# Decoder trunk on one core: the chunked RWKV recurrence with one engine loop for its inverses and a scan over chunk states

## The reference, cut to what matters

```python
def step(s, inp):
    r_t, w_t, k_t, v_t, a_t, b_t = inp
    sa = jnp.einsum('nhvk,nhk->nhv', s, a_t)
    s = s * w_t[:, :, None, :] + sa[..., None] * b_t[:, :, None, :] + v_t[..., None] * k_t[:, :, None, :]
    return s, jnp.einsum('nhvk,nhk->nhv', s, r_t)
...
mu_y = jnp.mean(y, axis=-1, keepdims=True)
var_y = jnp.mean(jnp.square(y - mu_y), axis=-1, keepdims=True)
y = ((y - mu_y) * lax.rsqrt(var_y + RWKV_GN_EPS)).reshape(n, t, RWKV_W)
y = y * lp['rwkv_ln_w'] + lp['rwkv_ln_b']
...
y_rwkv = ((y + bonus.reshape(n, t, RWKV_W)) * g).astype(h.dtype)
```

## Time and profile before

| what | us |
|---|---|
| median of three runs | 2193.56 |
| profiled execution, its own time | 2205.53 |
| its span | 2203.7 |
| PE busy | 2126.8 (97%) |
| first gram, to first product of the output projection | 1192.74 to 1318.54 |

### The profile page before, as it was taken

How to read it: one execution, slowest core, us unless ns; L and a number is a source line. 1 busy time by engine, 2 the same in 40 slices (tenths; PEclk the granted TensorE clock), 3 DMA queues, 4 the chain that set the end, 5 groups by cost and what they waited for, 6 DMA issues and landing times.

```text
span 2203.7 us, 46115 instructions
## 1 busy us (share of the span) xinstructions
PE 2126.8 (97%) x19116; PEld 2095.9 (95%) x19116; DVE 1191.8 (54%) x1232; ACT 857.5 (39%) x954; POOL 194.6 (9%) x158
## 2 busy tenths in 40 slices
PE   6999999999999999999987889999999999999997
PEld 5999999999999999999985779999999999999997
DVE  5555555555455454769766446555555555544442
ACT  4444444444344343443323114444444444433332
POOL 3000000000000010044104720100000000000000
PEclk9999999999999999999997859999999999999998
DMA  5555555555555556587850105655555555555552
GB/s 158 183 180 182 180 181 181 181 180 182 172 182 188 174 186 189 163 224 230 255 160 9 32 24 175 188 180 180 178 185 179 183 179 181 182 165 194 189 170 97
DMA packets 359032, 373.52 MB, mean 169 GB/s; under 512 B 13329, under 2 KB 351797, under 8 KB 358742
## 3 DMA queue, kind: packets, MB, share of 16 engines
q1 hardware_dynamic: 349280, 348.17, 49.7%
q0 software_dynamic: 5920, 17.48, 3.1%
q10 hardware_dynamic: 3742, 6.52, 0.9%
HBM read 366.82 MB, written 5.32 MB: 169 GB/s over the span
## 4 chain that ended last, share of the span: by engine, by line
PE 91%; DVE 5%; DMA 2%; ACT 1%; issue 1%; ACTq 0%; POOL 0%; SPq 0%; POOLq 0%; DVEq 0%
PE ps L305 28%; PE ps L307 28%; PE ps L306 28%; DMA raw<-in_w_in_dram 2%; DVE wL L292 1%; PE ps L1066 1%; PE ps L1394 1%; PE ps L1609 1%; PE ps L1582 1%; PE ps L1678 0%; DVE xL L339 0%; PE ps L1601 0%; ACT wH L286 0%; PE ps L1665 0%; PE ps L1760 0%
## 5 line engine op out<-in xcount | busy, mean ns | idle before, releaser
L292 DVE TENSOR_TENSOR wL<-raw,wH 128x1024 fp32r<-128x1024 f32 (+1 forms) x676 | 828.4, 1231 | 864.1 <-ACT wH L286 863.8
L286 ACT ACTIVATE wH<-raw 128x1024 fp32r<-128x1024 f32 (+1 forms) x676 | 699.9, 1037 | 1013.5 <-PE ps L307 948.2
L305 PE MATMUL ps<-xH,wH 128*128 128x264 f32 x3616 | 1031.8, 285 | 12.6 <-DVE wL L292 12.6
L307 PE MATMUL ps<-xH,wL 128*128 128x264 f32 x3616 | 1029.7, 285 | 0.0
L306 PE MATMUL ps<-xL,wH 128*128 128x264 f32 x3616 | 1029.5, 285 | 0.0
L305 PEld LDWEIGHTS ps<-xH,wH 128*128 128x128 f32 x3616 | 683.9, 189 | 14.6 <-issue 13.9
L307 PEld LDWEIGHTS ps<-xH,wL 128*128 128x128 f32 x3616 | 683.5, 189 | 0.0
L306 PEld LDWEIGHTS ps<-xL,wH 128*128 128x128 f32 x3616 | 683.0, 189 | 0.2
L305 PE MATMUL ps<-hH,wH 128*128 128x264 f32 x1408 | 402.4, 286 | 0.0
L307 PE MATMUL ps<-hH,wL 128*128 128x264 f32 x1408 | 401.4, 285 | 0.0
L306 PE MATMUL ps<-hL,wH 128*128 128x264 f32 x1408 | 401.3, 285 | 0.0
(11 more groups left out here) (331 smaller groups left out, 1219.2 us busy)
## 6 DMA issues: line engine op xcount, KB each, us to landing
raw<-in_ffn_w_gate_dram SPq DMA_DIRECT2D x176, 512.0 KB, 3.4
raw<-in_ffn_w_up_dram SPq DMA_DIRECT2D x176, 512.0 KB, 3.5
raw<-in_ffn_w_down_dram SPq DMA_DIRECT2D x128, 512.0 KB, 3.5
raw<-in_w_in_dram SPq DMA_DIRECT2D x100, 512.0 KB, 4.8
raw<-in_ffn_w_down_dram SPq DMA_DIRECT2D x64, 384.0 KB, 3.1
raw<-in_w_out_dram SPq DMA_DIRECT2D x32, 512.0 KB, 4.6
kb<-in_cache_swa_k_dram POOLq DMA_DIRECT2D x24, 256.0 KB, 6.5
vb<-in_cache_swa_v_dram ACTq DMA_DIRECT2D x24, 256.0 KB, 5.4
```

Of the source, the lines that this page charges most:

```text
L286: nc.scalar.activation(wH[:, k % RING, 0:nk, :], raw[:, k % RING, 0:nk, :], ACT.Copy).then_inc(S("head_made"), 1)
L292: nc.vector.tensor_tensor(wL[:, k % RING, 0:nk, :], raw[:, k % RING, 0:nk, :], wH[:, k % RING, 0:nk, :].bitcast(F32), ALU.subtract).then_i ...
L305: nc.tensor.matmul(out, wH[:, k % RING, q, cols], high, start=a, stop=False)
L307: last = nc.tensor.matmul(out, wL[:, k % RING, q, cols], high, start=False, stop=b)
```

## The change

- `inner` is one tile whose slots replace the separate tiles, since the loop needs fixed places and one product takes two of them side by side as its right operand.
- The levels become `with pe.Fori(0, LEVELS)` on TensorE alone; the other engines' level code stays unrolled. X is no longer kept by a product and a masked copy: every level TensorE transposes Z (6 transposes of 128x128) and VectorE copies the result.
- The chunk walk becomes: multiply the inverse with [own values | a by token] (`pe_solved`), form for chunks 1 to 3 a matrix that takes the incoming state to reads and to the next state (`pe_transition`), and then scan the states (`pe_state`) and write outputs for two chunks at a time (`pe_outputs`).
- Group norm has two parts. The gain is multiplied into the spread matrix `hs` once (GpSimd), the bias is added to the bonus by ScalarE, and both gates are on VectorE, in PSUM.
- GpSimd forms the sample output from the old state (one product by w r, and two dot products that VectorE reduces) before it updates the state. `ycat` and `sample_y` are now GpSimd's.

```diff
+    Zq = Wq = inner_slots(0, 1)
+    Aak = Fq = inner_slots(2, 3)
+    Xq = [m.rearrange("p (i t) c -> p i t c", t=2) for m in inner_slots(4, 7)]
+    FQ_AT, TOKA_AT = (2, 3), (5, 6)
+    toka = inner_slots(*TOKA_AT)
+    Aq = inner_slots(8, 9)
+    Qq = inner_slots(10, 11)
+    UV = inner_slots(12, 13, 14) + [last_uv[:]]
+    KB_AT, AR_AT = (11, 8, 9, 10), (5, 4, 7, 6)
+    KB, AR = inner_slots(*KB_AT), inner_slots(*AR_AT)
+    states = [inner[:, k:k + RT, :] for k in (2 * H, 2 * H + RT, 3 * H)] + [ST[:]]
+    LR = at("LR", [P, 3, RT, 2 * C], F32, PB)
...
+        pool.dma_start(lnwr[:], t["rwkv_ln_w"].broadcast_to([H, RW])).then_inc(S("rwkv_tables_in"), 16)
...
+        g.tensor_tensor(ycat[:], sv[:, 2:4, :], sv[:, 4:5, :].broadcast_to([96, 2, C]), ALU.mult
+                        ).then_inc(S("sample_parts"), 1)
+        step(g.tensor_tensor(sv[:, 0, :], sv[:, 1, :], sv[:, 4, :], ALU.mult))
+        pool.wait_ge(S("sample_sums"), 1)
         step(g.tensor_tensor(S2[:], S1[:], key(0), ALU.mult))
         halve()
         step(g.tensor_tensor(S1[:], S1[:], key(1), ALU.mult))
-        pool.wait_ge(S("sample_sums"), 1)
+        pool.wait_ge(S("sample_sums"), 3)
+        for value, dot in ((smal[:, 0:C], smal[:, C:C + 1]), (sv[:, 5, :], smal[:, C + 1:C + 2])):
+            step(g.tensor_scalar(ycat[:, 0, :], value, dot, None, ALU.mult))
+            step(g.tensor_tensor(smy[:], smy[:], ycat[:, 0, :], ALU.add))
+        for a in range(2):
+            g.tensor_scalar(ycat[:, a, :], smy[:], cgat[:, 48 + a:49 + a], None, ALU.mult).then_inc(S("sample_y"), 1)
...
+    def pe_inverse(pe):
+        pe.wait_ge(S("decayed"), 2)
+        pe.wait_ge(S("tokens_staged"), 5)
+        pe_gram(pe, bT, aT, 0, 0)
+        pe_gram(pe, aT, bT, 0, 4)
+        pe.wait_ge(S("tokens_staged"), 6)
+        pe_gram(pe, bT, aT, 1, 2)
+        pe_gram(pe, aT, bT, 1, 6)
+        pe.wait_ge(S("decayed"), 4)
+        for n in range(2):
+            pe.wait_ge(S("grams_out"), 2 * n + 1)
+            pe_gram(pe, pkr, aT, n, 4 + 2 * n)
+        with pe.Fori(0, LEVELS) as lv:
+            for n in range(2):
+                pe.wait_ge(S("grams_out"), 2 * n + 2)
+                pe.wait_ge(S("z_level"), lv * 2 + (n + 1))
+                for i in range(RT):
+                    pair = Zq[n][:, 2 * i:2 * i + 2, :].rearrange("p b c -> p (b c)")
+                    last = nc.tensor.transpose(wide(slice(0, P), 4 + 2 * n, i), pair, ident)
+                last.then_inc(S("level_x"), 1)
+                for i, b, cp in every():
+                    last = nc.tensor.matmul(place(HALF[b], 2 * n + cp, i), Aq[n][HALF[cp], slot(b, i), :],
+                                            Zq[n][HALF[cp], 2 * i + b, :], start=True, stop=True)
+                last.then_inc(S("level_q"), 1)
+            for n in range(2):
+                pe.wait_ge(S("grams_out"), 4)
+                pe.wait_ge(S("level_q_out"), lv * 2 + (n + 1))
+                pe.wait_ge(S("level_x_out"), lv * 2 + (n + 1))
+                for i, b, cp in every():
+                    last = nc.tensor.matmul(place(HALF[cp], 2 * n + b, i), Xq[n][HALF[b], i, cp, :],
+                                            Qq[n][HALF[b], slot(cp, i), :], start=True, stop=True)
+                last.then_inc(S("level_z"), 1)
...
+    def pe_solved(pe, m, first):
         for i, b, cp in every():
...
+            R = HALF[cp]
+            rhs = side_by_side(R, FQ_AT[m] * H + slot(b, i), TOKA_AT[m] * H + 2 * i + b)
+            last = nc.tensor.matmul(wide(HALF[1 - cp], first, 2 * i + b), Zq[m][R, 2 * i + b, :], rhs,
+                                    start=True, stop=True)
+        last.then_inc(S("solved"), 1)
+    def pe_turn_keys(pe, n, first):
+        c = chunk(n)
+        for i in range(RT):
+            low, high = (bT, pkr) if n % 2 else (pkr, bT)
+            nc.tensor.transpose(wide(HALF[0], first, i), low[:, i, c], ident)
+            last = nc.tensor.matmul(wide(HALF[1], first, i), high[:, i, c], ident, start=True, stop=True)
+        last.then_inc(S("tokens_turned"), 1)
+    def pe_reads(pe, n, first):
+        c = chunk(n)
+        for i in range(RT):
+            for k in range(4):
+                b, own = k % 2, k // 2 ^ k % 2
+                last = nc.tensor.matmul(place(HALF[n % 2 if own else 1 - n % 2], first + b, i),
+                                        (pkr if own else bT)[HALF[b], i, c], pr[HALF[b], i, c], start=True, stop=True)
+        last.then_inc(S("grams_made"), 1)
+    def pe_transition(pe, n, first):
+        m, R = n // 2, HALF[1 - n % 2]
+        for i, b in both():
+            rhs = side_by_side(R, AR_AT[n] * H + slot(b, i), KB_AT[n] * H + 2 * i + b)
+            last = nc.tensor.matmul(wide(HALF[b], first, i), Wq[m][R, 2 * i + b, :], rhs, start=True, stop=True)
+        last.then_inc(S("transitions"), 1)
+    def pe_state(pe, n, bank):
+        for i, b in both():
+            h, out = 2 * i + b, place(HALF[b], bank, i)
+            last = nc.tensor.matmul(out, KB[n][:, h, :], UV[n][:, h, :], start=True, stop=n == 0)
+            if n:
+                last = nc.tensor.matmul(out, LR[HALF[b], n - 1, i, C:2 * C], states[n - 1][HALF[b], i, :],
+                                        start=False, stop=True)
+        last.then_inc(S("states_made"), 1)
+    def pe_outputs(pe, m, first):
+        for n in (2 * m, 2 * m + 1):
+            for i, b in both():
+                h, k = 2 * i + b, i % 3 * P + n % 2 * C
+                out = ps[HALF[b], first + i // 3, k:k + C]
+                last = nc.tensor.matmul(out, UV[n][:, h, :], AR[n][:, slot(b, i), :], start=True, stop=n == 0)
+                if n:
+                    last = nc.tensor.matmul(out, states[n - 1][HALF[b], i, :], LR[HALF[b], n - 1, i, 0:C],
+                                            start=False, stop=True)
+        last.then_inc(S("outputs"), 1)
...
+        pe_own_values(pe, 0, 4)
+        pe_own_values(pe, 1, 6)
+        pe.wait_ge(S("z_level"), 11)
+        pe_reads(pe, 1, 0)
+        pe.wait_ge(S("z_level"), 12)
+        pe_turn_keys(pe, 1, 2)
+        pe.wait_ge(S("tokens_staged"), 8)
+        pe_solved(pe, 0, 4)
+        pe.wait_ge(S("tokens_staged"), 9)
+        pe_turn_keys(pe, 0, 2)
+        pe.wait_ge(S("grams_out"), 5)
+        pe.wait_ge(S("tokens_staged"), 10)
+        pe_solved(pe, 1, 0)
+        pe.wait_ge(S("solved_v"), 3)
+        pe.wait_ge(S("solved_a"), 3)
+        pe_transition(pe, 1, 4)
+        pe_state(pe, 0, 7)
+        pe.wait_ge(S("solved_v"), 6)
+        pe.wait_ge(S("solved_a"), 6)
+        pe_reads(pe, 2, 0)
+        pe_turn_keys(pe, 2, 2)
+        pe.wait_ge(S("transitions_out"), 1)
+        pe.wait_ge(S("states_out"), 1)
+        pe_state(pe, 1, 6)
+        pe_reads(pe, 3, 4)
+        pe.wait_ge(S("tokens_staged"), 11)
+        pe_turn_keys(pe, 3, 2)
+        pe.wait_ge(S("grams_out"), 6)
+        pe_transition(pe, 2, 0)
+        pe.wait_ge(S("tokens_staged"), 12)
+        pe_reads(pe, 0, 2)
+        pe.wait_ge(S("transitions_out"), 2)
+        pe.wait_ge(S("states_out"), 2)
+        pe_state(pe, 2, 7)
+        pe.wait_ge(S("grams_out"), 7)
+        pe_transition(pe, 3, 4)
+        pe.wait_ge(S("grams_out"), 8)
+        pe_outputs(pe, 0, 0)
+        pe.wait_ge(S("transitions_out"), 3)
+        pe.wait_ge(S("states_out"), 3)
+        pe_outputs(pe, 1, 4)
+        pe_group_sums(pe, 0)
+        pe_state(pe, 3, 1)
+        pe.wait_ge(S("sample_y"), 2)
+        nc.tensor.matmul(ps[:, 7, 408:456], ycat[:].rearrange("p a e -> p (a e)"), cgat[:, 0:48],
+                         start=True, stop=True).then_inc(S("sample_turned_y"), 1)
+        pe_group_squares(pe, 0)
...
-        nc.vector.tensor_tensor(tiles(pvr, part), tiles(pvr, part), group_bank(part), ALU.mult
...
+        dve.wait_ge(S("gates_out"), 18 + RT)
+        link(v.tensor_tensor(out, out, tiles(pvr, part), ALU.mult), dve)
+        link(v.tensor_tensor(out, out, tiles(bv, part), ALU.add), dve)
+        v.tensor_tensor(out, out, tiles(gg, part), ALU.mult).then_inc(S("rwkv_made"), 1)
...
+        keys(0)
+        keys(1)
+        solved(0)
+        solved(1)
+        keys(2)
+        keys(3)
...
+        act_group_squares(act, 0)
+        act_group_root(act, 0)
         act_group_squares(act, 1)
         act_group_root(act, 1)
...
+        act_rwkv_head(act, 0)
+        act_rwkv_head(act, 1)
         act.wait_ge(S("sample_state_out"), 16)
```

```diff
         for lv in range(LEVELS):
             for n in range(2):
+                dve.wait_ge(S("level_x"), 2 * lv + n + 1)
+                v.tensor_copy(Xq[n].rearrange("p (g i) t c -> p g (i t c)", g=2), ps[:, 4 + 2 * n:6 + 2 * n, 0:384]
+                              ).then_inc(S("level_x_out"), 1)
+            for n in range(2):
                 dve.wait_ge(S("level_z"), 2 * lv + n + 1)
...
+                dve_level(dve, 2 * (lv + 1) + n)
             if lv == 1:
-                dve_sample_sums(dve, 1)
+                dve.wait_ge(S("sample_parts"), 1)
```

(25 more changed lines are left out.)

483 lines of the change are left out of this document (149 added, 334 removed).

## The result

The changed kernel takes 2229.89 us (median of 4, 2228.79 to 2230.43), the kernel before 2191.62 in the same session (2188.53 to 2202.67). The ratio is 1.0165, with a 95% interval from 1.0128 to 1.0201: it is slower, since the whole interval lies above 1. The forecast was 2169.6, the range 2160 to 2194; both missed. The profiled execution took 2229.53 us, its span is 2227.8. One thing is needed to read the numbers: of 21 executions of the kernel before in the first session of experiments, 17 took 2186.6 to 2196.2 us and 4 took 2205.4 to 2207.1, and the one that was profiled before (2205.53) is like those four.

The account below looks back on a forecast made before the run. TensorE, busy for 97% of the span, was taken as the bound; levels 17 us less, chunks 33 us for 50, and the output projection's shift less 2 us kept back gave 24 us gain: 2169.6 us, range 2160 to 2194.

Parts of the forecast that it names:

- The grams and the levels: Inverse stage: no gain in grams, levels start at 1200, 5.8 to 5.9 us each, end at 1230.5; 17 us less.
- rival 3: Levels' loop: clock falls there too, 9.9 us a level, on top of a slow chunk stage; 2216, slower; chance 0.06.
- Rival 2: Levels' loop: code is fetched again at each back edge, 14 us; gain 10, total 2184; chance 0.06.
- The Trainium skill's rule on taken branches: Levels' loop: a taken branch with its target outside the two pages held stalls for a fetch; rows spoke against it.
- The chunks: Chunk stage: batches priced by rows, sum 32.3 us and 1 of waits, 33 in place of 50; outputs end at 1263.7.
- The keys: Chunk stage, six transposes beside six products: 1.6 us a batch taken, 2.3 if in turn; four batches, 6.4 us.
- The last state: Group norm stage: the last state was priced at 2.6 us, at half clock.
- The clock: Full clock forecast for the chunk stage, since batches alternate halves or use all rows; half clock for the norm.
- rival 1: Chunk stage: clock stays at half, 32.3 us grow by 25, 2193, chance 0.10; in part 2176 to 2190, chance 0.20.
- The norm and GpSimd: After the outputs: norm chain ends at 1293.4, GpSimd's at 1294.1, so together; first output product at 1294.3.
- The base: Whole kernel: gain of 24 us from the profiled 2205.5 us, carried over to the median 12 us below it: 2169.6.
- rival 4: Chunk stage: keys and solved at their lower bounds, GpSimd's and the norm's chains 3 us forward; 2165; chance 0.06.

Follow-up runs that it names:

- a1: Changed kernel with the 64-row product ahead of the 128-row one for every second head in states and outputs; 2188.33 us, ratio 0.9976 to the kernel before.
- a4: a3 with each keys batch issued as six transposes and then six products, instead of in turn; 2179.54 us, ratio 0.9921 to the kernel before.
- b2: Changed kernel without accumulation in states and outputs, same order of products (other numbers computed); 2229.46 us, ratio 1.0162 to the kernel before.
- b5: a4 with VectorE's sum for the sample ahead of its second solved copies, two weight heads and a tail earlier; 2173.52 us, ratio 0.9912.
- d1: b5 with each keys batch made of twelve plain products in turn on the two column halves; 2172.45 us, ratio 0.9906 to the kernel before.
- d3: Changed kernel with products grouped in runs by row size in the states alone, outputs still in turn; 2202.74 us, ratio 1.0032 to the kernel before.
- b4: a4 with the five levels of the inverse unrolled in TensorE's program instead of looped; 2179.21 us, ratio 0.9933 to the kernel before.
- b1: Changed kernel with products on the state before replaced by repeats of the 128-row products in states and outputs (other numbers computed); 2182.83 us, ratio 0.9952.
- a3: Changed kernel with products in runs by row size, four in the states and up to eight in the outputs; 2181.82 us, ratio 0.9945.

## Why the prediction was wrong, point by point

**The grams and the levels: right in their times, not in the reason.** Start 1197.7 (forecast 1200), passes 5.4 to 6.3 us apart (5.8 to 5.9), end 1226.9 (1230.5). The clock stayed at 1.00 with transposes busy for 8.7 of the 29.2 us, so rival 3 did not come. It is no flat rule: in six of the other kernels (a1, a4, b2, b5, d1, d3) the clock was 0.50 for 6.8 us from about 1198, over the start of the levels, and rose with the same transposes under way (a4: 0.50 from 1199.3 to 1206.1, then 1.00). The groups of the changed kernel that answer to the earlier trace rows, from 1195 to 1228:

```profile
L1625 PE MATMUL ps<-inner 64*64 64x64 f32 x480 | 9.3, 222 | 0.0
L1633 PE MATMUL ps<-inner 64*64 64x64 f32 x480 | 9.0, 220 | 2.2 <-issue 1.3 <-ACT inner L1846 0.9
L1622 PE MATMUL ps<-cb,inner 128*128 128x128 f32 x60 | 8.7, 282 | 0.7 <-DVE inner L1892 0.3 <-issue 0.2
```

Rival 2 did not come either: 1.5 us of issue waits in five passes, and 4 instruction packets from 1200 to 1250. The Trainium skill's rule on taken branches (the page and section named in the prediction) gives no visible cost here, and unrolling (b4) is no slower. Of the 18.9 us by which the stage is shorter, 10.5 are TensorE's busy time (36.8 to 26.3) and 8.4 its idle time (11.3 to 2.9). In the busy time, 60 transposes (8.7 us) stand for 192 products (13.1 us), and grams that were busy for some 6 us between the levels have moved to other stages. Why the idle time went is not shown; my reading of it as code that arrives late was not borne out.

**The chunks: the step that failed.** "States 0.8 and twice 1.5, outputs 2.2 and 2.9, from 30 to 34 ns a row as in own values." The states took 0.9, 7.0 and 9.7, the outputs 30.4. Own values is a batch of one size, and the price held wherever the batch had one size (b1: 1.66 and 5.17). It did not hold for products in turn between 128 and 64 rows. Against the forecast of 1263.7 the outputs ended at 1310.2, 46.5 us late: states 13.8 (17.6 for 3.8), outputs 25.3, keys 10.2 (16.6 for 6.4), and all the rest -2.8. The keys failed in the same way; I took the lower of two prices because the two kinds "use different columns", and only plain products do so with gain. The last state, which stands in the norm, failed once more: 9.75 us for the 2.6 forecast.

**The clock: wrong, as a consequence.** "The new chunk stage alternates halves or uses all rows in nearly every batch. So I take the full clock for it." It fell at about 1253, inside state 1, and was 0.50 until about 1328. With runs of two (a1) it did not fall in this stage. The outputs end at 1310.2 there and at 1270.7 in a3, 39.5 us apart. Up to that point a3 has 34 changes fewer in the states and 61 in the outputs; 95 at 0.20 us are 19 us of drains, and the other 20 are the lower clock, on the drains and on all between them. This is rival 1's condition, but it scaled a sum without drains and came to 2193. One reading behind the choice was also off. Of the 14 us at 0.50 that the prediction calls products on 64 or fewer rows, 3.4 were products on all 128 rows (groups of the kernel before, 1160 to 1174):

```profile
L1394 PE MATMUL ps<-pj,lora 128*128 128x264 f32 x7 | 3.4, 670 | 0.0
```

Nor do changes of size explain every fall: the chunk walk of the kernel before was at 0.50 for 38 us with nearly all its products of 64x64. What brings the clock down in general stays open; shown is that in this stage grouping the sizes keeps it up.

**The norm and GpSimd: right, in part by luck.** The state left at 1283.7 (forecast 1284). The levels ended 3.6 us early, and the two keys batches ahead of the sample's sum cost 4.0 us more than I had; the two cancel. In a3, where the drains are nearly gone, the first output product comes at 1294.8 (forecast 1294.3), and it follows the state's transfer. The norm's chain was done at 1291.2 (forecast 1292.2): there all four keys cost 8 us more than I had, and the full clock in the norm gave as much back. The span of a3 is 25.4 us below that of before, where I had forecast 24.

**The base: wrong by 12 us.** "The median of the runs is 12 us below it, and the same gain gives 2169.6." a3 has the forecast gain against the profiled execution, but its median is 9 us below that of before, 2182. The profiled execution of before is one of the longer ones (above), and a3's ten executions, 2177.6 to 2185.1 us, have none such. So a part of the 24 us was a loss that most executions do not have. It lies in the stretch that the change rewrites: behind the 48th output product all profiles of this case need 875.8 to 876.2 us, and the first gram of before, at 1192.7, starts no later than in some of the others (1189.6 to 1193.4). And it goes with the clock. The mean granted clock was 0.974 or 0.975 in the four long executions and 0.980 to 0.987 in the 17 others; 0.009 less over 2200 us is some 40 us more at 0.50 in place of 1.00, by estimate. The profiled execution has 61.5 us at 0.50 in the rewritten stretch, two windows of TensorE:

```profile
1254.00:1295.00 41.00, 41.00 (x561) 0.50 0.13 40
1301.80:1322.30 20.50, 16.27 (x67) 0.50 0.21 62
```

Which batches keep the full clock in a shorter execution no profile shows. What was wrong is that a gain against the slowest kind of execution was taken for the median's. a3's 2182 lies inside the range, but 12 us above the forecast. (A slip in rival 4, on which nothing hangs: 3 us less give 2166.6 and not 2165.)

## What to carry to other kernels

Before pricing a batch of small products by a row, write down the rows and columns of each product in issue order and count the places where they change. Group by size as far as open accumulations allow: mirroring every second pair halves the changes without touching an accumulation. A gain that is worked out against a profiled execution belongs to that execution; when it lies outside most of the runs, part of the gain may be its own excess. Its mean granted clock, beside that of the other executions, tells which kind it is.
